# Forgetting attention's decay rows made once, and SBUF buffers moved to other addresses, in a three-block transformer kernel on one Trainium2 core

## The chip, the cores and the metric

The kernel runs on one core of a Trainium2 chip. The metric is the time of one execution on the device in microseconds (us), as a median of runs. TensorE (PE) has two levels of clock, 1.2 and 2.4 GHz; the profile shows which was granted. Beside it work VectorE (DVE), ScalarE (ACT), GpSimd (POOL) and the DMA queue of SyncE (SP).

## What is computed

One sequence of 256 tokens with 1024 channels passes through three transformer blocks in float32. Block A has dilated band attention of 16 heads, block B block-sparse causal attention (at 256 tokens plain causal attention), each followed by a gated MLP with a short convolution of width 3. Block C mixes three branches: forgetting attention with 8 heads of 64, a convolution branch, and a pooling branch. Each block ends with a gated MLP of width 2816. The part that the change rewrites is the decay in the forgetting attention:

```python
def forgetting_attention(q, k, v, fg_logit):
    log_f = jax.nn.log_sigmoid(fg_logit.astype(jnp.float32))
    cum = jnp.transpose(jnp.cumsum(log_f, axis=1), (0, 2, 1))
    ...
        s = jnp.einsum('bqhd,bkhd->bhqk', qb, kb).astype(jnp.float32) * ATT_SCALE
        s = s + cum[:, :, start:end, None] - cum[:, :, None, :end]
        s = jnp.where(ki <= qi, s, NEG)
        p = jax.nn.softmax(s, axis=-1).astype(vb.dtype)
```

The term of the query's own position is the same for all keys of a row and drops out of the softmax, so the kernel adds only minus the running sum over keys, per head.

## The kernel before

All weights arrive as 384 KB to 512 KB chunks of one stream, in the order of use, through a ring of six slots. ScalarE splits each chunk into a high part `w_hi` (`split_hi`, L362) and VectorE makes the rest `w_lo` (`split_lo`, L370), both in the type fp32r. A product of two float32 numbers is then three matmuls: high by high, low by high, high by low. The activations are split the same way: `xg` holds the normalised input's high and low halves side by side (x's split), `mix_hi` and `mix_lo` the branches' output, `g_hi` and `g_lo` (two buffers each) the gated product of the MLP.

Four kinds of matmul carry the kernel:

- the projections to queries, keys and values (`unit_chunk_pe`, L650 to L652): a slice of `xg` stands still, 384 columns of weights move;
- the MLP's up-projections (`project2_k`, L402 and L404): weights stand still, `xg` moves, 512 columns (both halves at once) and then 256. In the same step of the MLP follows
- the down-projection (L1707 to L1709): weights stand still, `g_hi`, `g_lo`, `g_hi` move, 256 columns each, 24 matmuls to a chunk;
- the output projections (L1189 to L1191), which have the same shape as the down-projection, with `mix_hi`, `mix_lo`, `mix_hi` moving.

The MLP's steps `j` alternate between two sets of buffers: an even step uses PSUM banks 0 and 1 and `g_hi0`, `g_lo0`, an odd one banks 2 and 3 and `g_hi1`, `g_lo1`. One step has 16 pairs of L402 and L404 and 24 matmuls of L1707 to L1709; there are 22 steps to an MLP and three MLPs.

The order of every engine's work is written out by hand. In block C, `att_c_pe`, `att_c_act` and `att_c_dve` walk through the 16 weight chunks n of the projections and hang the attention's work between them. `score_c_pe`, once for each of the four pairs of heads, first writes the decay into the score banks and then adds the scores (L763). Its core in the kernel before:

```python
        for h in range(2):
            for t in range(2):
                col = t * HEADS_C + 2 * pr + h
                ...
                for n, part in enumerate((fg_hi, fg_lo)):
                    nc.tensor.matmul(out, part[:, col:col + 1].broadcast_to([P, P]), tri[:, 0:3 * P - 2 * P * t],
```

One column of `fg_hi` (the logarithm of the forget gate, split into `fg_hi` and `fg_lo`), repeated 128 times, stands still, and the triangle `tri` of minus ones moves: 384 columns for the first 128 keys, 128 for the rest. That makes eight matmuls on L756 for a pair of heads.

Where a buffer lies in a partition of SBUF follows from the order and sizes in which the buffers are declared. The addresses in bytes modulo 1024 that matter here are, before: the weight slots 128 (all of them), `xg` and `mix_hi`, `mix_lo` 192, the four `g` buffers 256, and the attention's working buffers (`tokbuf`, `qkT`, `v_tok`, `prob`) 96 or 608.

Of the kernel before, what the change touches and what calls it, by code (L numbers as in the profile page):

```python
# [8 lines left out]
P = 128  # L9
D = 1024  # L10
TOK = 256
# [28 lines left out]
WARM_UP = 16  # L40
HALVES = 3
GAINS = 16
CHUNK = KT * P
UNIT = 3 * P
QCHUNK = 2 * UNIT
# [112 lines left out]
def build(nc, x_d, xa_d, stream_d, par_d, con_d, taps_d, out_d):  # L158
# [10 lines left out]
    def sem(name):  # L169
# [3 lines left out]
    w_raw = [sb(f"w_raw{s}", [P, CHUNK]) for s in range(RING)]  # L173
    w_hi = [sb(f"w_hi{s}", [P, CHUNK], F32R) for s in range(RING)]
    w_lo = [sb(f"w_lo{s}", [P, CHUNK], F32R) for s in range(RING)]
    x_all = sb("x_all", [P, GAINS + KT * TOK])
    xT = x_all[:, GAINS:GAINS + KT * TOK].rearrange("p (k t) -> p k t", t=TOK)
    xg = sb("xg", [P, KT, 2, TOK], F32R)
    xg_hi, xg_lo = xg[:, :, 0, :], xg[:, :, 1, :]
    mix_hi = sb("mix_hi", [P, KT, TOK], F32R)  # L180
# [1 line left out]
    par = sb("par", [P, N_PAR])  # L182
    con = sb("con", [P, N_CON])
    zero = sb("zero", [P, TOK], BF16)
    ln_x = sb("ln_x", [P, TOK])
    rms_r = sb("rms_r", [P, TOK])

# [34 lines left out]
    cv_h = [sb(f"cv_h{i}", [P, PADC + TOK + 2]) for i in range(2)]  # L222
    taps = sb("conv_taps", [P, N_TAPS])
    cv_s0 = sb("cv_s0", [P, SHIFTS * W_SHIFT])
    cv_shift = [[cv_s0[:, c * W_SHIFT:(c + 1) * W_SHIFT] for c in range(SHIFTS)],
                [v_tok[c][:, TOK:TOK + W_SHIFT] for c in range(3)] + [prob_t[:, 0, 2, 0:W_SHIFT]]]
    W_PL = POOL_PAD + TOK
# [27 lines left out]
    half_hi = sem("half_hi")  # L255
    half_lo = sem("half_lo")
    rest_in = sem("rest_in")
    pl_zeroed = sem("pl_zeroed")
    zeroed = sem("zeroed")
    acc_done = sem("acc_done")  # L260
    x_new = sem("x_new")
# [73 lines left out]
    fg_dve = sem("fg_dve")  # L335
    fg_act = sem("fg_act")
    fg_lo_done = sem("fg_lo_done")
    ln_pe = sem("ln_pe")
    ln_dve = sem("ln_dve")
    ln_act = sem("ln_act")  # L340
# [95 lines left out]
    def norm_gain(e, m):  # L436

        g = PAR_NORM + KT * e + m
        return x_all[:, m:m + 1] if e == 0 else par[:, g:g + 1]

    def first_hi_dve(eng):
        eng.wait_ge(x_first, 16)
# [284 lines left out]
    def score_pe(eng, st, pr, g):  # L727
# [10 lines left out]
                                        kk[lo:hi, g * TOK:g * TOK + (qt + 1) * P], start=True, stop=True)  # L738
        last.then_inc(a.score, 1)

    def score_c_pe(eng, pr):

        a, b = att[2], pr % 2
        q, kk = qkT[b]
        if pr > 0:
            eng.wait_ge(a.ptr, pr)
        else:
            eng.wait_ge(ln_act, 1)
        eng.wait_ge(tri_in, 1)
        eng.wait_ge(fg_lo_done, 1)  # L750
        for h in range(2):
            for t in range(2):
                col = t * HEADS_C + 2 * pr + h
                out = bank(S_BANK + h, 2 * P * t, 3 * P - 2 * P * t)
                for n, part in enumerate((fg_hi, fg_lo)):
                    nc.tensor.matmul(out, part[:, col:col + 1].broadcast_to([P, P]), tri[:, 0:3 * P - 2 * P * t],  # L756
                                     start=(t == 0 and n == 0), stop=False, skip_group_check=True)
        eng.wait_ge(a.qe, pr + 1)
        eng.wait_ge(a.ke, pr + 1)
        for qt in range(2):  # L760
            for h in range(2):
                lo, hi = HD * h, HD * h + HD
                last = nc.tensor.matmul(bank(S_BANK + h, qt * P, (qt + 1) * P), q[lo:hi, qt * P:(qt + 1) * P],  # L763
                                        kk[lo:hi, 0:(qt + 1) * P], start=False, stop=True, skip_group_check=True)
        last.then_inc(a.score, 1)
# [732 lines left out]
    def att_c_pe(eng):  # L1498
        for n in range(N_C):
            p, o = divmod(n, UCH)  # L1500
            unit_chunk_pe(eng, 2, n)
            if n == 1:
                conv_pe(eng, 0)
            if n == 2:
                conv_pe(eng, 1)
            if n == 3:
                ln_sum_pe(eng)
            if n == 4:
                ln_var_pe(eng)
            if o == 0 and p >= 3:  # L1510
                prob_t_pe(eng, 2, p - 3, 0)
            if o == 1 and p >= 2:
                score_c_pe(eng, p - 2)
            if o == 1 and p >= 3:
                pv_pe(eng, 2, p - 3)
            if n == 5:
                pool_mm_pe(eng)
            if n == N_C - 3:
                pw_pe(eng)
            if o == 3 and p >= 1:  # L1520
                if p == 1:
                    eng.wait_ge(side_lo, 2)
                if p == 3:
                    eng.wait_ge(side_lo, 4)
                qkt_pe(eng, 2, p - 1)
        p = PAIRS_C - 1
        out_first(eng, 2, 0, UPPER)
        prob_t_pe(eng, 2, p - 2, 0)
        out_first(eng, 2, 1, UPPER)
        score_c_pe(eng, p - 1)  # L1530
# [12 lines left out]
        out_first(eng, 2, 5, LOWER)  # L1543
        prob_t_pe(eng, 2, p, 0)
        out_first(eng, 2, 6, LOWER)
        pv_pe(eng, 2, p)
        out_second(eng, 2, 4, UPPER)
        out_first(eng, 2, 7, LOWER)
        out_second(eng, 2, 5, UPPER)
        out_second(eng, 2, 6, UPPER)  # L1550
        out_second(eng, 2, 7, UPPER)

    def att_c_act(eng):
        for n in range(N_C):
# [8 lines left out]
                prob_t_act(eng, 2, p - 3, 0)  # L1563
            if n == 5:
                ln_rsqrt_act(eng)
            if n == 8:
                forget_hi_act(eng)
            if o == 1 and p >= 1:
                norm_act(eng, 2, p - 1, 0, 4)
            if n == 6:  # L1570
# [37 lines left out]
    def att_c_dve(eng):  # L1608
        for n in range(N_C):
            p, o = divmod(n, UCH)  # L1610
            split_lo(eng, C_QKV + n + AHEAD)
            if n == 0:
                conv_shift_dve(eng, 1, 1)
# [4 lines left out]
            if n == 7:  # L1618
                forget_sigmoid_dve(eng)
            if n == 8:  # L1620
                forget_lo_dve(eng)
            if n == 4:
                ln_center_dve(eng)
            if o == 0 and p >= 1:
# [221 lines left out]
    def pre_act_f(eng):  # L1846

        for n in range(N_PRE):
            split_hi(eng, C_PRE + n + AHEAD_HI)
            if n == 2:  # L1850
                rows_act(eng, 4)
                cols_act(eng, 2)
                nc.scalar.activation(tri[:], con[:, CON_TRI:CON_TRI + 3 * P], ACT.Copy).then_inc(tri_in, 1)
            if n in (3, 5):
                t = n // 2 - 1
                eng.wait_ge(pre_out, 2 * t + 2)
                if t == 0:
                    nc.scalar.preload_act_table_set("sigmoid_and_others")
                nc.scalar.activation(cv_e[t], cv_b[t], ACT.Sigmoid).then_inc(pre_act, 1)
# [4 lines left out]
    def pre_dve_f(eng):  # L1864
# [6 lines left out]
        def out(n):  # L1871
            if n == 0:
                eng.wait_ge(x_r, ROW_NO[4])
            if n == 4:
                eng.wait_ge(pl_zeroed, 6)
            eng.wait_ge(tiles, C_PRE + n + 1)
            nc.vector.tensor_tensor(PRE_OUT[n], bank(PRE_BANK[n]), rms_r[:], ALU.mult).then_inc(pre_out, 1)

# [15 lines left out]
    def pool_zeroes(eng):  # L1894
        for t in range(2):
            for b in pl[t]:
                nc.gpsimd.memset(b, 0.0).then_inc(pl_zeroed, 1)

    def pre_pool_f(eng):

# [154 lines left out]
    with nc.Block() as block:  # L2055

        @block.sync
        def _(sp):
# [7 lines left out]
                sp.dma_start(w_raw[c][:, part], stream_d[c, :, part]).then_inc(half_in[c] if kk == 0 else w_loaded[c], 16)  # L2066

            def load_x(m, n, landed):
                part = slice(GAINS + m * TOK if m else 0, GAINS + (m + n) * TOK)
                sp.dma_start(x_all[:, part], xa_d[:, part]).then_inc(landed, 16)  # L2070

            load_x(0, 1, x_first)
            load_x(1, 1, x_in[0])
# [121 lines left out]
        def _(pool):  # L2195
            nc.gpsimd.memset(cv_h[0][:], 0.0).then_inc(zeroed, 1)
            nc.gpsimd.memset(cv_h[1][:], 0.0).then_inc(zeroed, 1)
            resid_pool(pool, 0)
            tables_pool(pool)
            att_a_pool(pool)  # L2200
# [166 lines left out]
```

## Time and profile before

| | |
|---|---|
| median of 3 runs | 1060.22 us (1059.83 to 1062.07) |
| profiled execution | 1060.19 us |
| its span | 1058.4 us |
| PE busy | 1053.8 us, 100% |
| PE weight loads busy | 981.7 us, 93% |
| DVE busy | 862.2 us, 81% |
| ACT busy | 685.9 us, 65% |
| POOL busy | 342.0 us, 32% |

The span goes from the first to the last instruction; 1.8 us of the execution lie around it. Matmuls overlap in the profile: an instruction's duration has its way through the array in it, so what one costs in a stream is read from the starts of two neighbours and not from its duration. Weight loads (PEld) run beside the matmuls.

### The profile page before, as it was taken

Reading aid. Unit: us, or ns where it says so; the run is one execution under the profiler, and the core shown is the slowest. Engines: PE = TensorE matmul, PEld = TensorE weight load, DVE = VectorE, ACT = ScalarE, POOL = GpSimd, SP = SyncE. Lnnn points to the kernel's source line nnn. Section 1 sums busy time; section 2 is a strip of 40 time slices with the busy share of each in tenths; the row PEclk is TensorE's granted clock in tenths of the full one; section 3 lists DMA queues with packets and bytes.
Section 4 is the critical chain, followed back from the end, with each engine's and each line's share of the span. In section 5 each row is a group of like instructions: output and inputs, shape, how many; then the busy total and the mean of one; then the engine's idle time right before and its main releaser. Section 6 shows DMA issues by size and latency. Waiting matters only on the chain.

```text
span 1058.4 us, 21208 instructions
## 1 busy us (share of the span) xinstructions
PE 1053.8 (100%) x7508; PEld 981.7 (93%) x7508; DVE 862.2 (81%) x1588; ACT 685.9 (65%) x1262; POOL 342.0 (32%) x368
## 2 busy tenths in 40 slices
PE   9999999999999999999999999999999999999998
PEld 8999999999999999999989899999998999999998
DVE  7877778877799888887777998888896769988886
ACT  7766676776766555576776665555686666655552
POOL 4312222121365333322122553333350025533331
PEclk9999999999999999999999999999999999999999
DMA  9644545455466555535453675555434436655541
GB/s 317 225 159 150 164 151 180 149 185 196 161 219 198 195 181 190 159 110 179 152 164 120 216 216 187 188 187 189 134 112 144 146 114 225 212 187 190 183 154 41
DMA packets 57749, 183.34 MB, mean 173 GB/s; under 512 B 6352, under 2 KB 9680, under 8 KB 57424
## 3 DMA queue, kind: packets, MB, share of 16 engines
q1 hardware_dynamic: 56816, 181.52, 52.7%
q8 instruction: 41, 0.67, 0.3%
q10 hardware_dynamic: 864, 0.92, 0.3%
q14 instruction: 28, 0.23, 0.1%
HBM read 181.36 MB, written 1.05 MB: 172 GB/s over the span
## 4 chain that ended last, share of the span: by engine, by line
PE 99%; DMA 0%; DVE 0%; ACT 0%; DVEq 0%; issue 0%
PE ps L402 23%; PE ps L404 12%; PE ps L650 10%; PE ps L652 9%; PE ps L651 9%; PE ps L1707 6%; PE ps L1709 6%; PE ps L1708 6%; PE ps L1189 2%; PE ps L1191 2%; PE ps L1190 2%; PE ps L584 1%; PE ps L809 1%; PE ps L854 1%; PE ps L783 1%; PE ps L821 1%
## 5 line engine op out<-in xcount | busy, mean ns | idle before, releaser
L370 DVE TENSOR_TENSOR w_lo<-w_raw,w_hi 128x1024 fp32r<-128x1024 f32 (+2 forms) x369 | 441.0, 1210 | 56.0 <-ACT w_hi L362 55.3
L362 ACT ACTIVATE w_hi<-w_raw 128x1024 fp32r<-128x1024 f32 (+2 forms) x369 | 354.1, 972 | 163.3 <-PE ps L404 136.6
L402 PE MATMUL ps<-xg,w_hi 128*128 128x512 f32 x1056 | 374.7, 396 | 0.0
L404 PE MATMUL ps<-xg,w_lo 128*128 128x256 f32 x1056 | 297.0, 281 | 0.0
L402 PEld LDWEIGHTS ps<-xg,w_hi 128*128 128x128 f32 x1056 | 198.6, 188 | 44.6
L404 PEld LDWEIGHTS ps<-xg,w_lo 128*128 128x128 f32 x1056 | 198.1, 188 | 0.1
L1829 POOL TENSOR_TENSOR prob_t<-prob_t,qkT 128x256 f32<-128x256 f32 x63 | 100.3, 1593 | 289.6 <-ACT prob_t L1752 289.6
L650 PE MATMUL ps<-w_hi,xg 128*128 128x384 f32 (+1 forms) x556 | 193.1, 347 | 0.0
L652 PE MATMUL ps<-w_hi,xg 128*128 128x384 f32 (+1 forms) x556 | 186.8, 336 | 0.0
L651 PE MATMUL ps<-w_lo,xg 128*128 128x384 f32 (+1 forms) x556 | 186.7, 336 | 0.0
L1707 PE MATMUL ps<-g_hi,w_hi 128*128 128x256 f32 x528 | 149.2, 283 | 0.0
L1709 PE MATMUL ps<-g_hi,w_lo 128*128 128x256 f32 x528 | 148.9, 282 | 0.0
L1708 PE MATMUL ps<-g_lo,w_hi 128*128 128x256 f32 x528 | 148.6, 281 | 0.0
L1823 POOL TENSOR_TENSOR qkT<-prob,rms_r 128x256 f32<-128x256 f32 x132 | 119.2, 922 | 19.0 <-DVE prob L1766 10.3
L1799 DVE SCALAR_TENSOR_TENSOR qkT<-qkT,par 128x255 f32<-128x255 f32 (+1 forms) x264 | 111.6, 476 | 4.3 <-ACT qkT L1745 4.2
L650 PEld LDWEIGHTS ps<-w_hi,xg 128*128 128x128 f32 x556 | 104.4, 188 | 3.4 <-issue 2.7
L651 PEld LDWEIGHTS ps<-w_lo,xg 128*128 128x128 f32 x556 | 104.5, 188 | 0.1
L652 PEld LDWEIGHTS ps<-w_hi,xg 128*128 128x128 f32 x556 | 104.3, 188 | 0.0
L1707 PEld LDWEIGHTS ps<-g_hi,w_hi 128*128 128x128 f32 x528 | 99.6, 189 | 2.7
L1745 ACT ACTIVATE qkT<-qkT,par 128x256 f32<-128x256 f32 x132 | 76.4, 597 | 37.6 <-POOL qkT L1823 37.4
L1708 PEld LDWEIGHTS ps<-g_lo,w_hi 128*128 128x128 f32 x528 | 99.7, 189 | 0.0
L1709 PEld LDWEIGHTS ps<-g_hi,w_lo 128*128 128x128 f32 x528 | 99.3, 188 | 0.0
(182 smaller groups left out, 1388.5 us busy)
## 6 DMA issues: line engine op xcount, KB each, us to landing
w_raw<-w_stream SPq DMA_DIRECT2D x228, 512.0 KB, 3.6
w_raw<-w_stream SPq DMA_DIRECT2D x137, 384.0 KB, 3.4
w_raw<-w_stream SPq DMA_DIRECT2D x4, 392.0 KB, 3.0
con<-consts SPq DMA_DIRECT2D x1, 1024.0 KB, 7.5
x_all<-x_t SPq DMA_DIRECT2D x4, 256.0 KB, 5.5
conv_taps<-taps SPq DMA_DIRECT2D x1, 1024.0 KB, 7.1
w_raw<-w_stream SPq DMA_DIRECT2D x4, 192.0 KB, 4.4
x_all<-x_a SPq DMA_DIRECT2D x3, 256.0 KB, 5.5
```

The source lines that it names most:

```text
L362: nc.scalar.activation(w_hi[s][:, 0:w], w_raw[s][:, 0:w], ACT.Copy).then_inc(w_hi_done, 1)
L370: nc.vector.tensor_tensor(w_lo[s][:, 0:w], w_raw[s][:, 0:w], w_hi[s][:, 0:w].bitcast(F32), ALU.subtract).then_inc(w_lo_done, 1)
L402: nc.tensor.matmul(bank(b, 0, 2 * TOK), w_hi[s][:, k * P:(k + 1) * P], xg[:, k, :, :].rearrange("p h t -> p (h t)"), start=(k == 0), stop= ...
L404: last = nc.tensor.matmul(bank(b), w_lo[s][:, k * P:(k + 1) * P], xg_hi[:, k, :], start=False, stop=(k == KT - 1), skip_group_check=True)
L650: nc.tensor.matmul(out, hi, wh, start=(k == 0), stop=False)
L651: nc.tensor.matmul(out, hi, wl, start=False, stop=False)
L652: last = nc.tensor.matmul(out, lo, wh, start=False, stop=(k == KT - 1))
L1707: nc.tensor.matmul(acc(m), wh, g_hi[b][:], start=first, stop=False, skip_group_check=True)
L1708: nc.tensor.matmul(acc(m), wh, g_lo[b][:], start=False, stop=False, skip_group_check=True)
L1709: last = nc.tensor.matmul(acc(m), wl, g_hi[b][:], start=False, stop=True, skip_group_check=True)
L1799: nc.vector.scalar_tensor_tensor(cv_s[b][s][:, k:TOK], up_s[b][s][:, 0:TOK - k], par_col(f, t, per, i, 4 * s + 2 - k), cv_s[b][s][:, k:TOK ...
L1823: nc.gpsimd.tensor_tensor(up_s[t % 2][s], up_sum[s], rms_r[:], ALU.mult).then_inc(F.up, 1)
```

## The change

Three things are done.

1. **Addresses.** `x_all` is declared larger (its contents start at 960 bytes into it), and an unused buffer `gap` of 736 bytes is declared after `zero`. The new buffers stand at the end. Modulo 1024, `xg`, `mix_hi` and `mix_lo` move from 192 to 128, the four `g` buffers from 256 to 928, the attention's working buffers from 96 or 608 to 768 or 256, `par` from 192 to 128, `con` from 64 to 0, `tri` from 256 to 928. The weight slots stay at 128.
2. **Decay.** `decay_pe`, at chunk n = 8, makes the eight heads' running sums once, as eight rows of 384 columns in bank `K_BANK`: a block of eight columns of `fg_hi` or `fg_lo` stands still and `tri` moves. ACT copies them to `decay_hi` (fp32r), DVE makes the rest `decay_lo`. `score_c_pe` then picks a head's row with `head_row`, the first eight columns of the identity, one of which is repeated 128 times and stands still while all 384 columns of `decay_hi` and then `decay_lo` move: four matmuls for a pair of heads.
3. **Order.** `forget_hi_act` moves from n = 8 to n = 7 on ACT and `forget_lo_dve` to the front of n = 8 on DVE; `decay_act` and `decay_dve` come in at n = 8. Two memsets of 128x384 stand at POOL's start, one small copy (`head_row`) in ACT's work before block C's attention, and the semaphore `pl_zeroed` is merged into `zeroed`.

The diff, cut to its core:

```diff
+X0 = TOK
+GAP = 184
-    x_all = sb("x_all", [P, GAINS + KT * TOK])
-    xT = x_all[:, GAINS:GAINS + KT * TOK].rearrange("p (k t) -> p k t", t=TOK)
+    x_all = sb("x_all", [P, X0 + KT * TOK])
+    xT = x_all[:, X0:X0 + KT * TOK].rearrange("p (k t) -> p k t", t=TOK)
     zero = sb("zero", [P, TOK], BF16)
+    sb("gap", [P, GAP])
     cv_s0 = sb("cv_s0", [P, SHIFTS * W_SHIFT])
+    head_row = sb("head_row", [P, HEADS_C], F32R)
+    decay_hi = sb("decay_hi", [P, 3 * P], F32R)
+    decay_lo = sb("decay_lo", [P, 3 * P], F32R)
+    def decay_pe(eng):
+
+        eng.wait_ge(tri_in, 1)
+        eng.wait_ge(fg_lo_done, 1)
+        eng.wait_ge(att[2].ke, 1)
+        for t in range(2):
+            for n, part in enumerate((fg_hi, fg_lo)):
+                last = nc.tensor.matmul(bank(K_BANK, 2 * P * t, 3 * P - 2 * P * t)[0:HEADS_C, :],
+                                        part[:, t * HEADS_C:(t + 1) * HEADS_C], tri[:, 0:3 * P - 2 * P * t],
+                                        start=(t == 0 and n == 0), stop=False, skip_group_check=True)
+        last.then_inc(decay, 1)
+
+    def decay_act(eng):
+        eng.wait_ge(decay, 1)
+        eng.wait_ge(zeroed, 4)
+        nc.scalar.activation(decay_hi[0:HEADS_C, :], bank(K_BANK, 0, 3 * P)[0:HEADS_C, :], ACT.Copy).then_inc(decay, 1)
+
+    def decay_dve(eng):
+        eng.wait_ge(decay, 2)
+        nc.vector.tensor_tensor(decay_lo[0:HEADS_C, :], bank(K_BANK, 0, 3 * P)[0:HEADS_C, :],
+                                decay_hi[0:HEADS_C, :].bitcast(F32), ALU.subtract).then_inc(decay, 1)
     def score_c_pe(eng, pr):
-        eng.wait_ge(tri_in, 1)
-        eng.wait_ge(fg_lo_done, 1)
+        eng.wait_ge(decay, 3)
         for h in range(2):
-            for t in range(2):
-                col = t * HEADS_C + 2 * pr + h
-                out = bank(S_BANK + h, 2 * P * t, 3 * P - 2 * P * t)
-                for n, part in enumerate((fg_hi, fg_lo)):
-                    nc.tensor.matmul(out, part[:, col:col + 1].broadcast_to([P, P]), tri[:, 0:3 * P - 2 * P * t],
-                                     start=(t == 0 and n == 0), stop=False, skip_group_check=True)
+            col = 2 * pr + h
+            for n, part in enumerate((decay_hi, decay_lo)):
+                nc.tensor.matmul(bank(S_BANK + h, 0, 3 * P), head_row[:, col:col + 1].broadcast_to([P, P]), part[:],
+                                 start=(n == 0), stop=False, skip_group_check=True)
```

On PE, after the projections' chunk n = 9 (L650 to L652 before), the first pair of heads' decay stands like this in the kernel before:

```order
L652 MATMUL ps<-w_hi,xg 128x384
L756 MATMUL ps<-tri,fg_hi 128x384
L756 MATMUL ps<-tri,fg_lo 128x384
L756 MATMUL ps<-tri,fg_hi 128x128
L756 MATMUL ps<-tri,fg_lo 128x128
L756 MATMUL ps<-tri,fg_hi 128x384
L756 MATMUL ps<-tri,fg_lo 128x384
L756 MATMUL ps<-tri,fg_hi 128x128
L756 MATMUL ps<-tri,fg_lo 128x128
L763 MATMUL ps<-qkT 128x128 x2
L763 MATMUL ps<-qkT 128x256 x2
```

In the changed kernel (whose L656 to L658 are the projections) the same place and, before it, the end of chunk n = 8 read:

```order
L658 MATMUL ps<-w_hi,xg 128x384
L754 MATMUL ps<-tri,fg_hi 8x384
L754 MATMUL ps<-tri,fg_lo 8x384
L754 MATMUL ps<-tri,fg_hi 8x128
L754 MATMUL ps<-tri,fg_lo 8x128
L656 MATMUL ps<-w_hi,xg 128x384
...
L781 MATMUL ps<-decay_hi,head_row 128x384
L781 MATMUL ps<-decay_lo,head_row 128x384
L781 MATMUL ps<-decay_hi,head_row 128x384
L781 MATMUL ps<-decay_lo,head_row 128x384
L788 MATMUL ps<-qkT 128x128 x2
```

Eight matmuls for a pair have become four, and four have come in once, a chunk earlier.

On DVE, between the keys of pair 0 and the norms of pair 1, the kernel before has (L370 the weights' split, L1004 and L1018 the norms):

```order
L1033 TENSOR_SCALAR qkT<-ps,gain_qk 128x256
L370 TENSOR_TENSOR w_lo<-w_raw,w_hi 128x768
L991 TENSOR_TENSOR fg_lo<-fg,fg_hi 128x16
L1004 TENSOR_REDUCE ss_q<-tokbuf 128x4 x2
L370 TENSOR_TENSOR w_lo<-w_raw,w_hi 128x768
L1018 SCALAR_TENSOR_TENSOR tokbuf<-ps,r_c,r_q 128x256 x2
```

And the changed kernel:

```order
L1058 TENSOR_SCALAR qkT<-ps,gain_qk 128x256
L1016 TENSOR_TENSOR fg_lo<-fg,fg_hi 128x16
L376 TENSOR_TENSOR w_lo<-w_raw,w_hi 128x768
L766 TENSOR_TENSOR decay_lo<-ps,decay_hi 8x384
L1029 TENSOR_REDUCE ss_q<-tokbuf 128x4 x2
L376 TENSOR_TENSOR w_lo<-w_raw,w_hi 128x768
L1043 SCALAR_TENSOR_TENSOR tokbuf<-ps,r_c,r_q 128x256 x2
```

The small `fg_lo` has moved ahead of a split, and `decay_lo` stands ahead of the sums. ACT changes likewise: its `fg_hi` copy moves up by one chunk, and `decay_hi` takes its old place.

## Rows read from the trace of the kernel before

**Rows 1.** The page: span, busy time, share and instructions of engines, granted clock, chain.

```profile
span 1058.4 us, 21208 instructions
PE 1053.8 (100%) x7508; PEld 981.7 (93%) x7508; DVE 862.2 (81%) x1588; ACT 685.9 (65%) x1262; POOL 342.0 (32%) x368
...
PEclk9999999999999999999999999999999999999999
...
PE 99%; DMA 0%; DVE 0%; ACT 0%; DVEq 0%; issue 0%
```

**Rows 2.** Groups on PE by form: busy us, mean ns of one, idle before.

```profile
L650 PE MATMUL ps<-w_hi,xg 128*128 128x384 f32 x540 | 187.5, 347 | 0.0
...
L1707 PE MATMUL ps<-g_hi,w_hi 128*128 128x256 f32 x528 | 149.2, 283 | 0.0
...
L1189 PE MATMUL ps<-mix_hi,w_hi 128*128 128x256 f32 x192 | 55.5, 289 | 0.0
```

**Rows 3.** Timeline of PE at pair 0's decay: start us, us, what.

```profile
815.03 0.34 PE L756 MATMUL ps<-tri,fg_hi 128*128 128x384 f32 x1
815.21 0.33 PE L756 MATMUL ps<-tri,fg_lo 128*128 128x384 f32 x1
815.38 0.22 PE L756 MATMUL ps<-tri,fg_hi 128*128 128x128 f32 x1
815.44 0.27 PE L756 MATMUL ps<-tri,fg_lo 128*128 128x128 f32 x1
815.55 0.39 PE L756 MATMUL ps<-tri,fg_hi 128*128 128x384 f32 x1
...
816.22 0.93 PE L763 MATMUL ps<-qkT 64*128 64x128 f32 x8
```

**Rows 4.** Timeline of ACT in block C's attention.

```profile
776.14 0.51 ACT L1853 ACTIVATE tri<-con 128x384 fp32r<-128x384 f32 x1
...
811.15 0.85 ACT L362 ACTIVATE w_hi<-w_raw 128x768 fp32r<-128x768 f32 x1
...
813.43 0.64 ACT L893 ACTIVATE v_tok<-ps,r_c 128x128 f32<-128x128 f32 x2
813.93 0.24 ACT L987 ACTIVATE fg_hi<-fg 128x16 fp32r<-128x16 f32 x1
814.04 0.87 ACT L362 ACTIVATE w_hi<-w_raw 128x768 fp32r<-128x768 f32 x1
...
818.63 0.40 ACT L950 ACTIVATE prob<-prob,nmax 128x128 f32<-128x128 f32 x1 [2.17 <-DVE nmax L1094]
```

**Rows 5.** Timeline of DVE in the same stretch.

```profile
812.03 0.96 DVE L370 TENSOR_TENSOR w_lo<-w_raw,w_hi 128x768 fp32r<-128x768 f32 x1 [0.49 <-ACT w_hi L362]
...
814.30 0.74 DVE L1004 TENSOR_REDUCE ss_q<-tokbuf 128x4 f32<-128x256 f32 x2
...
817.19 0.29 DVE L1087 CUSTOM_DVE_ANT_0 prob<-ps,con 128x128 f32<-128x128 f32 x1 [0.50 <-PE ps L763]
```

**Rows 6.** Windows of the first MLP: ups, down, ups, down of two steps.

```profile
305.11:310.77 5.66, 5.66 (x35) 4.93 (x34) 5.39 (x9) 2.99 (x6) 3.77 (x3) 1.00 0.76 224
310.77:313.64 2.87, 2.87 (x26) 2.87 (x25) 2.87 (x5) 2.13 (x3) 1.54 (x1) 1.00 0.40 134
313.64:319.24 5.60, 5.60 (x35) 4.90 (x33) 5.35 (x9) 3.53 (x6) 2.83 (x3) 1.00 0.78 260
319.24:322.08 2.84, 2.84 (x27) 2.84 (x25) 2.84 (x4) 1.68 (x3) 2.39 (x2) 1.00 0.42 131
```

**Rows 7.** Timeline of PE in block B's output projection.

```profile
553.40 0.28 PE L1190 MATMUL ps<-mix_lo,w_hi 128*128 128x256 f32 x1
...
556.01 0.60 PE L723 MATMUL ps<-con,tokbuf 128*128 128x128 f32 x4
```

**Rows 8.** Timeline of PE in block C's output projection.

```profile
852.84 0.28 PE L1189 MATMUL ps<-mix_hi,w_hi 128*128 128x256 f32 x1
...
857.79 0.82 PE L840 MATMUL ps<-con,prob 128*128 128x128 f32 x6
```

More of the change, by code:

```diff
@@ L257, in build @@
     rest_in = sem("rest_in")
-    pl_zeroed = sem("pl_zeroed")
     zeroed = sem("zeroed")
@@ L337, in build @@
     fg_lo_done = sem("fg_lo_done")
+    decay = sem("decay")
     ln_pe = sem("ln_pe")
@@ L438, in norm_gain @@
         g = PAR_NORM + KT * e + m
-        return x_all[:, m:m + 1] if e == 0 else par[:, g:g + 1]
+        return x_all[:, X0 - GAINS + m:X0 - GAINS + m + 1] if e == 0 else par[:, g:g + 1]
     def first_hi_dve(eng):
@@ L1517, in att_c_pe @@
                 pool_mm_pe(eng)
+            if n == 8:
+                decay_pe(eng)
             if n == N_C - 3:
@@ L1565, in att_c_act @@
                 ln_rsqrt_act(eng)
+            if n == 7:
+                forget_hi_act(eng)
             if n == 8:
-                forget_hi_act(eng)
+                decay_act(eng)
             if o == 1 and p >= 1:
@@ L1610, in att_c_dve @@
             p, o = divmod(n, UCH)
+            if n == 8:
+                forget_lo_dve(eng)
             split_lo(eng, C_QKV + n + AHEAD)
@@ L1620, in att_c_dve @@
             if n == 8:
-                forget_lo_dve(eng)
+                decay_dve(eng)
             if n == 4:
@@ L1852, in pre_act_f @@
                 cols_act(eng, 2)
+                nc.scalar.activation(head_row[:], con[:, CON_ID:CON_ID + HEADS_C], ACT.Copy)
                 nc.scalar.activation(tri[:], con[:, CON_TRI:CON_TRI + 3 * P], ACT.Copy).then_inc(tri_in, 1)
@@ L1874, in out @@
             if n == 4:
-                eng.wait_ge(pl_zeroed, 6)
+                eng.wait_ge(zeroed, 10)
             eng.wait_ge(tiles, C_PRE + n + 1)
@@ L1896, in pool_zeroes @@
             for b in pl[t]:
-                nc.gpsimd.memset(b, 0.0).then_inc(pl_zeroed, 1)
+                nc.gpsimd.memset(b, 0.0).then_inc(zeroed, 1)
     def pre_pool_f(eng):
@@ L2068, in load_x @@
             def load_x(m, n, landed):
-                part = slice(GAINS + m * TOK if m else 0, GAINS + (m + n) * TOK)
-                sp.dma_start(x_all[:, part], xa_d[:, part]).then_inc(landed, 16)
+                a, b = GAINS + m * TOK if m else 0, GAINS + (m + n) * TOK
+                sp.dma_start(x_all[:, X0 - GAINS + a:X0 - GAINS + b], xa_d[:, a:b]).then_inc(landed, 16)
             load_x(0, 1, x_first)
@@ L2197, in _ @@
             nc.gpsimd.memset(cv_h[1][:], 0.0).then_inc(zeroed, 1)
+            nc.gpsimd.memset(decay_hi[:].bitcast(F32), 0.0).then_inc(zeroed, 1)
+            nc.gpsimd.memset(decay_lo[:].bitcast(F32), 0.0).then_inc(zeroed, 1)
             resid_pool(pool, 0)
```

## The prediction

> **What bounds the kernel now.** The page first: PE is busy for 1053.8 of 1058.4 us, the chain that ended last is PE for 99%, and the granted clock is in the top tenth (2.4 GHz) in every slice [rows 1]. Nothing that another engine does sets the time unless it makes PE wait. So only two things can move it: which matmuls PE has, and how far apart they start. For the second, durations are no use (283 ns for a 256-column matmul of L1707, [rows 2]), since they overlap; starts are. In the first MLP, 24 down matmuls take 2.87 us in one step and 2.84 us in the next, 119.6 and 118.3 ns each, and the 16 pairs of up matmuls 5.66 and 5.60 us, 353.8 and 350.0 ns a pair [rows 6]. 256 columns at 2.4 GHz are 106.7 ns, so each down matmul carries 12 to 13 ns beyond its columns; a pair's 768 columns are 320 ns, and it carries 30 to 34 ns. Over the program that is some 20 us in the down matmuls (three MLPs times 22 steps times 24 are 1584) and some 34 us in the 1056 pairs. These are what an address could touch.
>
> **The change part by part, the decay.** Before, pair 0's eight decay matmuls start at 815.03 and the scores at 816.22: 1.19 us; the first four steps are 0.18, 0.17, 0.06 and 0.11 us [rows 3]. The new block has four of 384 columns. Three steps at 0.175 make 0.525 us; the last step, into the scores, whose stationary operand sits on half the rows, costs more than its columns: before it was the eighth of the block, and what the first seven leave of 1.19 us (0.52 for the first four, some 0.46 for the next three, whose first starts at 815.55) is 0.21 us for a 128-column matmul. With 384 columns instead I add the 0.107 us of 256 columns at least nothing (if the load of the weights sets that step) and at most all of it: 0.21 to 0.32, I take 0.27. The block is then 0.80 us, against 1.19: 0.39 saved, four times: 1.6 us, between 1.4 and 1.8.
>
> The four new `decay_pe` matmuls have the same columns as the first four of the old block, with only eight columns of weights to load: 0.52 us by those rows, 0.43 (1024 columns at 2.4 GHz) at the least. Net of the decay: minus 1.1 us, bounds minus 0.9 to minus 1.4.
>
> **The waits it adds.** `score_c_pe` waits for `decay_lo` on DVE, which waits for `decay_hi` on ACT, which waits for PE. Worked forward: chunk n = 9 runs for twelve matmuls of 384 columns, 2.1 us at 0.174, up to 815.03, so n = 8 ends at 812.95. `fg_hi` now follows the split that begins at 811.15 and takes 0.85 [rows 4], so it is there at 812.2 and `fg_lo` at 812.4, 0.5 us ahead of `decay_pe`. That ends at 813.45 plus 0.2 of its own way through the array. ACT is at its v copies until 814.0 then, and puts `decay_hi` where the 0.11 us of `fg_hi` were; a 128x384 copy took 0.51 us at L1853 [rows 4]: 814.5. DVE is idle from there for nothing else; a 128x768 subtraction took 0.96 [rows 5], so 384 columns about 0.55: 815.1. Chunk 9 ends 0.5 us later than before, at 815.5. PE has 0.4 us in hand. I cost the wait at nothing; if both copies ran as long as their 768-column rows (0.85 and 0.96) it would be short by some 0.3 us, once.
>
> Behind these two instructions things slide. DVE's sums, before at 814.30 [rows 5], come at 815.1; the split behind them and the norms then end some 0.8 to 0.9 us later, and the masks, which before started at 817.19 after 0.50 us of idle time, start near 817.6. ACT's exponentials, which had waited 2.17 us for that maximum [rows 4], begin 0.4 us later. The split now late is that for chunk 12, which PE reaches after 821, and ACT and DVE have idle time in between. Nothing on PE. The memsets at POOL's start and the 0.1 us of `head_row` on ACT lie under work that PE does not wait for.
>
> **The change part by part, the addresses.** No instruction is added, so only the steps between starts can change. What bears on whether they depend on an address: the output projections have the same shape as the down matmuls, three matmuls of 256 columns on two weight loads of the same slots, and differ in that their moving operand lies at 192 modulo 1024, the MLP's at 256. In block C, 42 of them take 4.95 us, 117.9 ns each [rows 8]; in block B 23 take 2.61 us, 113.5 ns each [rows 7]. Two rates at one address: so history (how the stream was entered) sets it too. The up pairs also alternate between 353.8 and 350.0 ns at one address of x. But of the triples, those at 256 are the slowest on record, at 119.6 and 118.3, and this is the address given up. The 1620 projection matmuls of L650 to L652 (540 of L650, [rows 2]) move weights, which stay at 128, and only hold x still; I leave them alone.
>
> What 928 gives no row shows. The nearest rows are the other triples. If `g` ran at block C's 117.9, 1584 matmuls would save 1.1 ns each, 1.7 us; at block B's 113.5, 8.6 us; if all steps ran as the even ones, at 119.6, they would cost 1.0 us. I take 117.7, nearer the first row because it is twice as long and the next to the MLP in time: minus 2.0 us. For x at 128, all pairs at 350.0 would save 2.0 us, all at 353.8 would cost 2.0; I take nothing. Of the output projections (192 triples, 576 matmuls) nothing either, with bounds of 1 us each way.
>
> **The sum.** Against the profiled execution, 1060.19 us, of which 1058.4 are the span: minus 1.1 for the decay, minus 2.0 for the gated product: 1057.1 us. The median of the runs is 1060.22, so the same holds there.
>
> **The rivals.**
> (a) Only the decay is worth anything: the addresses don't reach PE. For it: two rates at one address, as above, and the MLP's pattern is as regular as if only the code set it. Time 1059.1. The Trainium skill has a rule for this case: its page "SBUF — State Buffer", section "Who interferes with whom", says that PE never waits on another engine, and "TensorE: Matmul & The Clock Gate", section "Step-by-step: what each phase is for", that the moving operand and the weight load have independent read ports. By these an address could not matter at all, and the sum would be this rival's.
> (b) The new addresses are slower. Two streams, moving and stationary, are read side by side; before, `g` stood 128 bytes above the weights modulo 1024 and x 64; now x stands level with them, and 928 is the only one that isn't a multiple of 64. If the pairs settle at 353.8 or above and the triples at 119.6 or above, that is 2.0 and 1.0 us; with each step 2 ns more besides, 5 us more. The time would be 1061 to 1067; it decides against me from 3.1 us of added steps, about 1.2 ns on each of the 2640 up steps and down matmuls. For it: nothing but that both are untried.
> (c) Both become faster: the pairs at 350.0 throughout and the triples at 115 or so, minus 2.0 and minus 6.4: 1050.7; for it the 113.5 in block B, against it that no MLP step shows it.
> (d) PE waits for `decay_lo`: a gap of up to 1 us in front of the first decay block, and the decay's gain is gone, 1058 to 1060 with the rest as it falls.
>
> **Chances and range.** A faster gated product, x unchanged: 0.42. (a): 0.26. (b): 0.18. (c): 0.10. (d): 0.04. What a measurement of this kernel can tell from no change is about 0.2%, 2.1 us. Faster by more than that are the forecast, nearly all of it, and (c): 0.51. Within are (a), (d) and a bit of (b): 0.32. Slower: 0.17. The range that leaves out 2 in 10 is 1052 to 1062.5 us: below it most of (c), above it most of (b). The forecast's own range is 1055 to 1058.1.
>
> **What would show it.** In the changed profile: the decay block four matmuls in 0.8 us from first start to the scores, `decay_pe` in 0.5, and no idle step ahead of either. In the MLPs, the 24 down matmuls of a step should take 2.80 to 2.84 us in place of 2.87 and 2.84, and the 16 pairs still 5.66 and 5.60. The prediction is wrong if the steps of the down matmuls stand as they were (then (a)), if the pairs move by more than 0.05 us a step, or if the first decay block is preceded by a gap.

## The result, and the profile after

The changed kernel takes 1054.28 us (median of 6 runs, 1054.01 to 1054.57), against 1061.21 us for the kernel before (6 runs, 1059.83 to 1062.57): ratio 0.9939, 95% interval 0.9929 to 0.9949. The profiled execution took 1054.57 us, its span 1052.8 us, 5.6 us less than before. The forecast was 1057.1 in a range of 1052.0 to 1062.5. Of the six runs of the kernel before, three took 1059.8 to 1060.4 us and three 1062.1 to 1062.6, while those of the changed kernel lie within 0.6 us; the profiled execution before is one of the faster three, which is why the medians are 6.9 us apart and the spans 5.6.

The page of the kernel after (span; busy time and share of each engine; granted clock in 40 slices; shares of the chain that ended last):

```profile
span 1052.8 us, 21191 instructions
PE 1047.9 (100%) x7496; PEld 977.1 (93%) x7496; DVE 864.5 (82%) x1589; ACT 687.4 (65%) x1264; POOL 345.0 (33%) x370
...
PEclk9999999999999999999999999999999999999999
...
PE 97%; DMA 1%; DVE 1%; ACT 0%; POOL 0%; issue 0%; SPq 0%; DVEq 0%; POOLq 0%
```

Against [rows 1], PE is still busy throughout, at the same granted clock in every slice (2.4 GHz), and its busy time fell by 5.9 us, as the span did by 5.6. The other engines do slightly more. PE's matmuls are only 12 fewer, so most of the gain must be in their spacing. The windows of two steps of the first MLP, pairs then down matmuls, show where (columns: window, length, busy time of PE, PEld, DVE, ACT and POOL, granted clock, DMA share, GB/s):

```profile
322.60:328.15 5.55, 5.55 (x34) 4.89 (x33) 5.30 (x8) 3.65 (x6) 2.41 (x3) 1.00 0.70 238
328.15:330.98 2.83, 2.83 (x26) 2.83 (x25) 2.83 (x5) 1.49 (x3) 2.75 (x3) 1.00 0.55 188
330.98:336.53 5.55, 5.55 (x34) 4.89 (x33) 5.31 (x8) 3.40 (x5) 2.48 (x2) 1.00 0.54 187
336.53:339.36 2.83, 2.83 (x26) 2.83 (x25) 2.83 (x4) 1.97 (x3) 2.75 (x3) 1.00 0.82 275
```

In [rows 6] the same windows were 5.66, 2.87, 5.60 and 2.84. The pairs, which the forecast left as they were, lost 0.11 and 0.05 us a step (346.9 ns a pair now), the down matmuls 0.04 and 0.01 (117.9 ns each), and the two steps no longer differ.

A matmul's cost is the time from its start to the next one's. Summed over each group (the small ones are left out):

| group (us) | before | after | change | forecast |
|---|---|---|---|---|
| up pairs (`project2_k`) | 372.06 | 367.87 | −4.19 | 0, bounds ±2.0 |
| down matmuls | 188.46 | 186.70 | −1.76 | −2.0 |
| block C's decay and scores (`score_c_pe`) | 8.15 | 6.58 | −1.57 | −1.6 |
| `decay_pe` | 0 | 0.47 | +0.47 | +0.52 |
| output projections | 70.04 | 71.30 | +1.26 | 0, bounds ±1 |
| block C's `project_k` (x moving, triples) | 18.36 | 18.63 | +0.27 | not named |
| projections with x at rest (`unit_chunk_pe`) | 298.68 | 298.74 | +0.06 | 0 |
| all matmuls | 1053.88 | 1048.25 | −5.63 | −3.1 |

The +0.06 of the projections with x at rest is made of two parts. Their last matmul ahead of block A's first transposes takes 0.46 us longer, because PE waits there for GpSimd, and all the others together take 0.40 us less:

```profile
29.99 0.87 PE L703 MATMUL ps<-con,tokbuf 128*128 128x128 f32 x6 [0.30 <-POOL tokbuf L1184]
```

The output projections are the group that lost most; on PE's timeline (start, duration, what), a matmul of block C's and the one that starts 45 steps later:

```profile
848.39 0.28 PE L1215 MATMUL ps<-mix_lo,w_hi 128*128 128x256 f32 x1
...
853.78 0.28 PE L1215 MATMUL ps<-mix_lo,w_hi 128*128 128x256 f32 x1
```

That is 5.39 us for 45 steps, 119.8 ns each, where [rows 8] gave 117.9: these matmuls, whose moving operand now lies level with the weights, run as slowly as the down matmuls did before.

The decay, on PE:

```profile
810.19 0.34 PE L754 MATMUL ps<-tri,fg_hi 128*8 128x384 f32 x1
810.36 0.33 PE L754 MATMUL ps<-tri,fg_lo 128*8 128x384 f32 x1
810.53 0.22 PE L754 MATMUL ps<-tri,fg_hi 128*8 128x128 f32 x1
810.59 0.22 PE L754 MATMUL ps<-tri,fg_lo 128*8 128x128 f32 x1
...
812.79 0.34 PE L781 MATMUL ps<-decay_hi,head_row 128*128 128x384 f32 x1
812.96 0.34 PE L781 MATMUL ps<-decay_lo,head_row 128*128 128x384 f32 x1
813.14 0.33 PE L781 MATMUL ps<-decay_hi,head_row 128*128 128x384 f32 x1
813.31 0.34 PE L781 MATMUL ps<-decay_lo,head_row 128*128 128x384 f32 x1
813.58 0.93 PE L788 MATMUL ps<-qkT 64*128 64x128 f32 x8
```

The block takes 0.79 us up to the scores (1.19 in [rows 3]), and no idle time is noted ahead of it. The load of its first weights and ACT's and DVE's parts of the same chain:

```profile
812.61 0.19 PEld L781 LDWEIGHTS ps<-decay_hi,head_row 128*128 128x128 f32 x1
```

```profile
811.27 0.46 ACT L762 ACTIVATE decay_hi<-ps 8x384 fp32r<-8x384 f32 x1
```

```profile
811.77 0.55 DVE L766 TENSOR_TENSOR decay_lo<-ps,decay_hi 8x384 fp32r<-8x384 f32 x1 [1.35 <-ACT decay_hi L762]
```

`decay_lo` is ready at 812.32. The block's first matmul starts at 812.79, but PE's wait stands in the program ahead of the matmul and its weight load, and that load starts at 812.61: 0.29 us in hand. DVE idles 1.35 us ahead of `decay_lo`, and no idle time of PE follows from it.

### The profile page after: what moved, and what is told of

Its sections match the earlier page's. It is cut to its first block, busy times and chain, and to the rows that moved or that the text cites. A ratio compares the mean times of both kernels' runs of the same rounds, so it can differ in the third digit from the quotient of the medians.

```text
span 1052.8 us, 21191 instructions
## 1 busy us (share of the span) xinstructions
PE 1047.9 (100%) x7496; PEld 977.1 (93%) x7496; DVE 864.5 (82%) x1589; ACT 687.4 (65%) x1264; POOL 345.0 (33%) x370
## 4 chain that ended last, share of the span: by engine, by line
PE 97%; DMA 1%; DVE 1%; ACT 0%; POOL 0%; issue 0%; SPq 0%; DVEq 0%; POOLq 0%
PE ps L408 23%; PE ps L410 12%; PE ps L656 9%; PE ps L658 9%; PE ps L657 9%; PE ps L1738 6%; PE ps L1739 6%; PE ps L1740 6%; PE ps L1214 2%; PE ps L1215 2%; PE ps L1216 2%; DMA w_raw<-w_stream 1%; PE ps L834 1%; PE ps L879 1%; PE ps L808 1%; PE ps L846 1%
## 5 line engine op out<-in xcount | busy, mean ns | idle before, releaser
L368 ACT ACTIVATE w_hi<-w_raw 128x1024 fp32r<-128x1024 f32 (+2 forms) x369 | 353.8, 972 | 152.6 <-PE ps L410 128.5
L408 PE MATMUL ps<-xg,w_hi 128*128 128x512 f32 x1056 | 370.4, 393 | 0.0
L656 PE MATMUL ps<-w_hi,xg 128*128 128x384 f32 (+1 forms) x556 | 192.6, 346 | 0.0
L658 PE MATMUL ps<-w_hi,xg 128*128 128x384 f32 (+1 forms) x556 | 186.4, 335 | 0.0
L656 PEld LDWEIGHTS ps<-w_hi,xg 128*128 128x128 f32 x556 | 104.5, 188 | 3.4 <-issue 2.7
L658 PEld LDWEIGHTS ps<-w_hi,xg 128*128 128x128 f32 x556 | 104.4, 188 | 0.0
```

The costliest lines, as they stand in the source:

```text
L368: nc.scalar.activation(w_hi[s][:, 0:w], w_raw[s][:, 0:w], ACT.Copy).then_inc(w_hi_done, 1)
L408: nc.tensor.matmul(bank(b, 0, 2 * TOK), w_hi[s][:, k * P:(k + 1) * P], xg[:, k, :, :].rearrange("p h t -> p (h t)"), start=(k == 0), stop= ...
L656: nc.tensor.matmul(out, hi, wh, start=(k == 0), stop=False)
L658: last = nc.tensor.matmul(out, lo, wh, start=False, stop=(k == KT - 1))
```

## The experiments

Positions below are bytes modulo 256 unless said otherwise; the weights stand at 128 if nothing else is said. After the result two questions are open: why the pairs moved, and whether what counts is where an operand lies or how far it lies from the other operand.

### The decay alone, and the addresses alone

`e1_decay` is the kernel before with all of the decay's edits and before's positions:

```diff
+X0 = GAINS
-    x_all = sb("x_all", [P, GAINS + KT * TOK])
+    x_all = sb("x_all", [P, X0 + KT * TOK])
...
+    head_row = sb("head_row", [P, HEADS_C], F32R)
+    decay_hi = sb("decay_hi", [P, 3 * P], F32R)
+    decay_lo = sb("decay_lo", [P, 3 * P], F32R)
```

> The decay rows alone, all buffers at the addresses of the kernel before. Sums are over the time from each matmul's start to the next one's start. Theory A (each kind of matmul stream has its own step, set by where its moving operand lies modulo 1024): score_c's matmuls with decay_pe fall by 1.1 us as in the changed kernel, up pairs stay at 372 us, down matmuls at 188.5, output projections at 70.0; ratio to before 0.999. Theory B (the phase of the stream is history, and any change of the program redraws it): up pairs and down matmuls move too, by 1 to 4 us. Theory C (the decay's new order on ACT and DVE brought part of the gain): ratio below 0.997.

`e2_addr` is the kernel before with the positions alone:

```diff
+X0 = TOK
+GAP = 184
...
     zero = sb("zero", [P, TOK], BF16)
+    sb("gap", [P, GAP])
```

> The addresses of the changed kernel with the decay of the kernel before. If the two parts add up: 1.1 us slower than the changed kernel, ratio to before 0.995; up pairs 368, down 186.7, output projections 71.3 us. If the new addresses only pay together with the new order: ratio above 0.997.

The decay alone: 1059.13 us, ratio 0.9994 (0.9985 to 1.0003), span 1057.1 against 1058.4. The interval takes in 1, so the time alone doesn't show this gain; PE's groups do. Its pairs take 372.01 us, its down matmuls 188.46, its output projections 70.02, all as before; `score_c_pe` 6.58 and `decay_pe` 0.47. The addresses alone: 1055.23 us, ratio 0.9951 (0.9937 to 0.9964), span 1053.6; pairs 367.92, down 186.70, output projections 71.32, `score_c_pe` 8.15. The spans are 1.3 and 4.8 us shorter, 6.1 in sum, where both parts together gave 5.6. The groups named here add up, each to within 0.1 us. Four fifths of the gain are the addresses.

### One distance at a time

`e3_x` keeps the new position of x and puts `g` back to 256 modulo 1024, that is 0 (x and mix lie ahead of `gap` and don't move with its size; the attention's working buffers and `tri` lie behind it and go back too):

```diff
-GAP = 184
+GAP = 16
```

> The changed kernel with the gap cut to 64 bytes: x's split and the mixed branches stay at 128 modulo 1024, the gated product and the attention's working buffers go back to 256 and 96. Theory A: up pairs stay at 368 us (before 372), output projections at 71.3 (before 70.0), down matmuls go back to 188.5 from 186.7; time 1.8 us above the changed kernel, ratio to before 0.9955. Theory B: up pairs at some third value. Theory D (the up pairs gained through the working buffers' or the gated product's addresses, since they follow the down matmuls and take over their phase): up pairs back at 372 and ratio 0.999.

`e4_g` has x and mix at 192 as before and `g` at 928 modulo 1024, that is 160:

```diff
-X0 = TOK
-GAP = 184
+X0 = GAINS
+GAP = 168
```

> The changed kernel with x's split and the mixed branches back at 192 modulo 1024, the gated product at 928 and the working buffers at 768 as in the changed kernel. Theory A: up pairs at 372 us, output projections at 70.0, down matmuls 186.7 as in the changed kernel; ratio to before 0.9975. Theory B: a third value for each. Theory D: up pairs at 368, ratio 0.994.

`e3_x` took 1060.73 us, ratio 1.0003 (0.9994 to 1.0012): the gain was gone, where the first theory had expected 0.9955. Its windows of pairs and down matmuls:

```profile
322.43:328.08 5.65, 5.65 (x35) 4.90 (x33) 5.40 (x9) 3.46 (x6) 2.50 (x3) 1.00 0.70 215
328.08:330.93 2.85, 2.85 (x27) 2.85 (x26) 2.85 (x4) 1.81 (x3) 2.77 (x3) 1.00 0.64 217
```

x's pairs stood at the new position and ran at 5.65, not at 5.55; over the program they took 372.95 us, 0.88 more than before. In the first steps of the MLP, ahead of the loop, they had run at 5.55 here too and then changed to 5.65. `e4_g` took 1057.83 us, ratio 0.9974 (0.9965 to 0.9983):

```profile
322.13:327.79 5.66, 5.66 (x35) 4.93 (x34) 5.40 (x9) 3.49 (x6) 2.51 (x3) 1.00 0.72 237
327.79:330.59 2.80, 2.80 (x27) 2.80 (x25) 2.80 (x4) 1.73 (x3) 2.72 (x3) 1.00 0.59 199
```

Its down matmuls were faster than after's (184.92 against 186.70 us in all), its pairs the slowest (373.93), where the first theory had 186.7 and 372. So neither stream has a cost that goes by its own position alone: of these four kernels only the one with x at 128 and `g` at 160 runs its pairs at 5.55, and what `g` at 160 gives depends on where x is. My reading, that the two moves could be costed apart, fell here.

### Distance or position

`e6_all64` moves everything by 64 bytes, weights too (weights 192, x 192, `g` 992):

```diff
+    sb("gap_all", [P, 16])
```

> The changed kernel with 64 unused bytes ahead of the first buffer, so that every buffer, the weights too, lies 64 bytes higher: x's split 192, gated product 992, weights 192. If distances between the streams' operands count: up pairs 368 us, down 186.7, output 71.3, ratio to before 0.994. If absolute addresses modulo 1024 count: up pairs 372 to 374, ratio 0.998 to 1.000.

It took 1054.08 us, ratio 0.994 (0.9927 to 0.9954), and three of PE's groups are those of the kernel after to the last digit: pairs 367.87, down 186.70, output projections 71.30.

```profile
322.07:327.62 5.55, 5.55 (x34) 4.89 (x33) 5.30 (x8) 3.66 (x6) 2.41 (x3) 1.00 0.77 248
327.62:330.45 2.83, 2.83 (x26) 2.83 (x25) 2.83 (x5) 1.49 (x3) 2.75 (x3) 1.00 0.48 181
```

x stands at 192 here, where it stood in the kernel before, and runs at 5.55. What counts is how the operands lie to each other and not where they lie; that was tested with this one shift.

`e5_mix` is after with mix back at 64 bytes above the weights, the rest as after:

```diff
-GAP = 184
+GAP = 168
+    sb("gap_mix", [P, 16])
```

> The changed kernel with a gap of 64 bytes ahead of the mixed branches: they lie at 192 modulo 1024 as in the kernel before, x's split at 128 and the gated product at 928. Theory A: output projections back from 71.3 to 70.0 us and all else as in the changed kernel, 1.3 us below it, ratio to before 0.9925. Theory B: up pairs or down matmuls move as well.

1053.39 us, ratio 0.9934 (0.992 to 0.9948), span 1051.8, 1.0 below after's. The output projections are back at 69.99 us, the pairs at 368.12 and the down matmuls at 186.61; `unit_chunk_pe` took 299.21, 0.47 more than after, of which 0.12 is the wait for GpSimd ahead of block A's first transposes; the rest nothing here explains. The change's largest loss was mix's move, and it can be undone by itself.

### PE alone

Four kernels leave the transformer out and have PE go through the MLP's streams with nothing beside it, on fixed buffers filled once. Each was executed once. Each case, that is each set of positions, begins with a matmul of four columns (`kick`). The core of the first three:

```python
            for xo, go in CASES:
                kick(xo)
                for j in range(STEPS):
                    pairs(xo, 2 * (j % 2), 0)
                    pairs(xo, 2 * (j % 2) + 1, 1)
                    down(go, j % 2, j % 2)
```

`map_g` has x at 128 and `g` at 0 to 992 modulo 1024 in steps of 32.

> PE alone: the kernel leaves the whole computation out and returns x. It runs the MLP's two streams (16 up pairs, 24 down matmuls a step, four steps) 32 times, x at 128 modulo 1024 and the gated product at 0, 32, ... 992, weights at 128, no other engine at work. Theory A' (the two streams' addresses and nothing else set the steps): at 928 a step has its up pairs in 5.55 us and down in 2.83, at 256 in 5.65 and 2.85, as the MLPs of the changed kernel and of the one with g back at 256. Rival (other engines' reads and writes of SBUF make the extra time): up pairs near 5.2 and down near 2.62 at every address, which is their columns plus 2.5 ns a matmul.

`map_x` has `g` at 928 modulo 1024 and x at 0 to 992.

> The same kernel, gated product at 928, x at 0, 32, ... 992 modulo 1024 (whole computation left out). Theory A': at 192 the pairs take 5.66 us a step and down 2.80, at 128 5.55 and 2.83. If only the distance from the weights (128) matters the values repeat in some pattern of 64 or 128 bytes. Rival: no dependence.

The page of `map_g` shows that nothing but PE works:

```profile
PE 1088.3 (98%) x7241; PEld 998.2 (90%) x7241; ACT 10.2 (1%) x9; POOL 0.2 (0%) x4
```

And its windows of one step each with `g` at 64, 256, 320 and 928 modulo 1024 (columns: window, length, busy time of PE, granted clock, DMA share, GB/s):

```profile
114.34:119.90 5.56, 5.56 (x35) 1.00 0.00 0
119.90:122.62 2.72, 2.72 (x26) 1.00 0.00 0
317.39:323.05 5.66, 5.66 (x35) 1.00 0.00 0
323.05:325.89 2.84, 2.84 (x26) 1.00 0.00 0
384.73:390.28 5.55, 5.55 (x34) 1.00 0.00 0
390.28:393.01 2.73, 2.73 (x26) 1.00 0.02 6
1026.92:1032.47 5.55, 5.55 (x35) 1.00 0.01 3
1032.47:1035.30 2.83, 2.83 (x27) 1.00 0.00 0
```

At 928 it gives after's 5.55 and 2.83, at 256 `e3_x`'s 5.65 and 2.85 to 0.01 us, without any other engine. So neither the other engines nor the working buffers that moved with `g` are needed for the effect. Adding 256 bytes changes nothing (64 and 320). The last step of each case, ns from the first start of a part to the next part's:

```
position of the one that varies      0    32    64    96   128   160   192   224
map_g (x at 128): 16 pairs        5653  5639  5554  5547  5651  5552  5649  5552
                  24 down         2847  2819  2726  2835  2882  2828  2828  2881
map_x (g at 928): 16 pairs        5600  5552  5651  5546  5551  5547  5657  5600
                  24 down         2815  2801  2829  2808  2829  2800  2803  2827
```

(Some cases alternate from step to step, and the last step stands here: the step before, `map_g` at 32 had pairs at 5552, at 192 down at 2721, and `map_x` at 96 had pairs at 5644. For `map_x` at 0 the middle of two values stands here: 5608 and 2805 at 0 modulo 1024, 5595 and 2825 at 256, 512 and 768.)

`map_xg` takes eight positions of x times eight of `g`, three steps each.

> PE alone (whole computation left out, returns x): x and gated product each at the eight multiples of 32 in 256 bytes, three steps for each of the 64 cases. If each stream has a time of its own, a row and a column of the first two maps predict every cell: x at 128 pairs 5.55, gated product at 64 down 2.73, and no cell below 8.25 us a step. If the streams hand over a phase to each other, cells with the same gated product differ in their down time by 0.02 to 0.1 us.

Its windows of the third step for (x, g) = (32, 64), (160, 64) and (192, 0), the last being the kernel before's:

```profile
303.51:309.08 5.57, 5.57 (x41) 1.00 0.00 0
309.08:311.81 2.73, 2.73 (x18) 1.00 0.00 0
1117.61:1123.17 5.56, 5.56 (x41) 1.00 0.00 0
1123.17:1125.99 2.82, 2.82 (x20) 1.00 0.02 6
1269.48:1275.14 5.66, 5.66 (x40) 1.00 0.00 0
1275.14:1278.01 2.87, 2.87 (x20) 1.00 0.00 0
```

The down matmuls at one position of `g` take 2.73 after x at 32 and 2.82 after x at 160: a stream's rate also depends on the one that it follows. Of the 64 combinations x at 128 with `g` at 64 is the least in the third step, 8280 ns; the largest is 8536. The kernel before's combination has 8535 there, but 8432 in the second step: pairs and down matmuls take 5657 and 2878 ns in the one and 5594 and 2838 in the other. These are the two kinds of step of [rows 6] (5.66 and 2.87, 5.60 and 2.84), so PE alone shows both kinds of step, at one position of x and of `g`.

`map_m` runs the triples of the down matmuls alone, then uniform streams of 256, 384 and 512 columns with new weights for each matmul, then the projections' stream with x at rest. In a triple the first two matmuls have the same weights, but PE loads weights for each of the three (`map_g`'s page counts as many loads as matmuls, 7241).

> PE alone (whole computation left out, returns x), eight positions of the moving operand in 256 bytes: the triple of the down matmuls by itself, uniform streams of 256, 384 and 512 columns with one new load of weights for each matmul, and the projections' stream, where weights move and x holds still. If the extra time comes from the moving operand's distance to the weights being loaded, the triple by itself takes 113 to 114 ns a matmul at 64 and 118 to 120 at 128, and the uniform streams vary with position too; the projections' stream does as well, since the distance is the same seen from the other side. If it comes from the moving operand's own alignment, the projections' stream is the same at all eight.

Windows of 24 matmuls of the triples with `g` at 64 (the first two), 128 and 160:

```profile
136.89:139.61 2.72, 2.72 (x26) 1.00 0.00 0
139.61:142.33 2.72, 2.72 (x26) 1.00 0.00 0
236.78:239.66 2.88, 2.88 (x26) 1.00 0.00 0
285.36:288.16 2.80, 2.80 (x26) 1.00 0.00 0
```

ns for one matmul, by position of `g` or x, with the weights at 128:

```
position                   0      32      64      96     128     160     192     224
above the weights by     128     160     192     224       0      32      64      96
triples, 256 columns   120.0   118.6   113.3   118.3   120.0   116.7   117.8   120.0
uniform, 256           118.6   117.4   117.8   118.4   120.0   116.6   117.8   119.9
uniform, 384           176.4   176.7   173.4   173.3   173.3   176.6   173.3   176.7
uniform, 512           232.2   234.3   233.3   233.4   226.7   233.3   228.9   233.2
x at rest, 384         176.0   176.7   173.3   173.3   173.3   173.3   174.7   173.3
```

The triples keep such a value step after step, but another start of the same stream can settle on another one: with `g` at 64 it took 2826 ns per 24 at another start (2720 at the first), at 0 it took 2849 (2880). The two rates that the forecast noted at one address in [rows 7] and [rows 8], 113.5 and 117.9 ns, look like this. The full kernels show it too: with mix at 192 in all three, 48 matmuls in a row of block B's output projection took 115.7 ns each in `e5_mix`, as in the kernel before, and the same 48 took 119.9 in `e4_g`.

### The positions that the map prefers

`e7_best` leaves x at 128 and puts mix and `g` at 64 (the working buffers move along, to 160):

```diff
-GAP = 184
+GAP = 176
+    sb("gap_mix", [P, 48])
```

> The changed kernel with the mixed branches at 64 and the gated product at 64 modulo 256 (x stays at 128, weights at 128). If the map of PE alone holds in the full kernel (period 256 bytes, down matmuls in 2.73 us a step instead of 2.83 where the gated product lies at 64, up pairs 5.55): down matmuls 180 us instead of 186.7, output projections, which are the same triple, 68 instead of 71.3, up pairs 368; time 1044, ratio to before 0.985. Rival (the changed kernel's addresses are good because of 928 or of the working buffers that moved with them, and the map doesn't carry over with other engines at work): 1054 or above.

1047.63 us (4 runs, 1047.6 to 1048.57), ratio 0.9881 (0.9864 to 0.9897): faster than both kernels, 6.6 us below after. Its windows of a step:

```profile
322.14:327.70 5.56, 5.56 (x35) 4.90 (x33) 5.30 (x9) 3.70 (x6) 2.61 (x3) 1.00 0.73 262
327.70:330.43 2.73, 2.73 (x27) 2.73 (x26) 2.73 (x4) 1.61 (x3) 2.36 (x2) 1.00 0.39 134
```

Down matmuls took 180.47 us in all, 6.2 less than after, and output projections 68.69, 2.6 less. The time missed the expectation of 1044 by 3.6 us, and part of that is a new wait. On the weight loads' timeline at the start of the third MLP:

```profile
861.36 0.19 PEld L409 LDWEIGHTS ps<-xg,w_hi 128*128 128x128 f32 x1 [0.37 <-DVE xg L474]
...
862.41 0.19 PEld L409 LDWEIGHTS ps<-xg,w_hi 128*128 128x128 f32 x1 [0.40 <-DVE xg L474]
...
863.65 0.19 PEld L409 LDWEIGHTS ps<-xg,w_hi 128*128 128x128 f32 x1 [0.59 <-DVE xg L474]
```

PE comes to the MLP before VectorE has made x's low halves. The waits' summary has six such waits:

```profile
PEld ps L409 <- DVE xg L474: 2.7, 6, 0.6
```

From the first pair of the second and of the third MLP to the next step's first pair it takes 7.03 us in place of 5.90, so 2 times 1.13 us are lost there; without them the pairs' 369.91 us would be 367.65. Against the kernel after, `unit_chunk_pe` took 0.57 us more (299.31 us), of which 0.35 is the wait for GpSimd ahead of block A's first transposes. Against the expected 368, 180 and 68, the pairs (with these waits), the down matmuls and the output projections are 1.9, 0.5 and 0.7 us too long; with the projections' 0.57 that makes the 3.6. But the trace is that of the slowest of the four executions, 1 us above the other three, and no trace shows what those did otherwise.

## Why the prediction was right, and where a step of it failed

**What bounds the kernel.** Right: PE is the chain for 97%, and the time between its matmuls' starts fell by 5.63 us in sum, as the span did by 5.6.

**The decay.** Right: block of 0.79 us (0.80 forecast), `decay_pe` 0.47 (0.52), net −1.1 (−1.1), and −1.1 again on PE's groups in `e1_decay`. The wait for `decay_lo` cost nothing, as forecast; counted to the weight load it had 0.29 us in hand and not 0.4. Rival (d) did not come.

**The gated product.** −1.76 against −2.0, at 117.9 ns in place of the 117.7 that I chose from block C's row. The size was right by luck: it was taken from a row with its moving operand 64 bytes above the weights, and `g` went to 32 above; by `e4_g` the same address of `g` gives 2.80 us a step (116.7 ns) with x at 192. The working also says that a triple has two weight loads, where the page of the kernel before has as many loads as matmuls (7508); the sum doesn't use it.

**x's pairs.** This is the term that failed: costed at nothing, with bounds of 2.0 us each way taken from the two rates of [rows 6]; they gave −4.2. But for the first steps of each MLP's loop, the pairs now run below both of those rates (346.9 ns against 350.0 and 353.8). The bound was wrong in kind: two rates seen at one distance say nothing about another distance. It was also wrong to cost the streams one by one, as `e3_x` and `e4_g` show. By the prediction's own sign (wrong if the pairs move by more than 0.05 us a step) this part of it was wrong: the even steps moved by 0.11.

**The output projections.** Costed at nothing with bounds of 1 us, +1.26: just outside, for the same reason. `e5_mix` takes it back with mix alone.

**The sum.** −3.1 forecast, −5.6 measured. What was not in the forecast is pairs −4.2, output projections +1.3, `project_k` +0.3, and the gated product is 0.2 short. The errors partly cancel, and the time stayed in the range of 1052 to 1062.5; it lies below the forecast's own range, which ended at 1055. The direction was right, but the largest part of the size, the pairs' −4.2, came from a term that stood at nothing, so that the time is in the range is in part luck.

**The rivals.** (a), that addresses do not reach PE, is refuted by `e2_addr` (−4.8 us of span with no instruction added or taken out) and by the maps. The Trainium skill says on its page "SBUF — State Buffer", section "Who interferes with whom", that the ports for the matmul's moving operand and for the weight load are independent. For these fp32r streams it can't be concluded from this, as (a) did, that an address doesn't matter: the step depends on where the two operands lie to each other, 113.3 to 120.0 ns for 256 columns. Whether the ports themselves are independent no run here shows. The same section says that PE never waits on another engine. Of the access to SBUF, which that section is about, the trace agrees for the MLP's steps: PE alone has the same 5.55 and 2.83 us as in the full kernel. (b) put its doubt on x standing level with the weights; with `g` at 160 that is a good place for the pairs (5.55 us), and for the triples one of the worst (120.0 ns in `map_m`), which is what the output projections met. (c) had the right sign for both streams; it put the pairs at 350.0 ns and the triples at 115, and they came to 346.9 and 117.9.

**What stays open.** Shown is that the spacing goes with how the two operands lie to each other, with a period of 256 bytes, in PE alone; that it is the distance, and not the position, rests on `e6_all64`'s one shift of 64 bytes. Only multiples of 32 bytes were tried. Which part of the hardware makes it so was not measured, nor why a stream can settle on more than one value, nor why half of the kernel before's runs took 2 us more.

## What to carry to other kernels

Where PE is the chain from end to end, divide a regular stretch of matmuls by their count of starts: if the steps differ between places that have the same shape, try where the moving buffers lie against the weights, modulo 256 bytes, with an unused buffer of 16 to 48 words, and measure all streams that alternate together and not one by one. Price such a move by measuring PE's stream alone and not from the rates seen at other distances. Then look at the start of each stage, since PE, once faster, can find the next engine's work not ready.

## What the runs showed of the hardware

- At 2.4 GHz (granted clock 1.00), fp32r matmuls with new weights followed at 116.6 to 120.0 ns for 256 columns, 173.3 to 176.7 for 384, 226.7 to 234.3 for 512, by the distance of the moving operand from the stationary one; in triples, where two of three matmuls have the same weights, 256 columns had 113.3 to 120.0.
- The period is 256 bytes: `map_g` gives the same values at 64 and at 320 (5.55 and 2.73 us).
- Moving both operands by 64 bytes changes nothing (`e6_all64`: pairs 367.87 us, as after).
- With weights moving and x at rest it is seen as well, 173.3 to 176.7 ns for 384 columns (`map_m`).
- A stream's rate depends on the one that it follows (2.73 and 2.82 us for the same 24 matmuls in `map_xg`), and the same stream can settle on two rates at one distance (2720 and 2826 ns per 24 in `map_m`).
- PE loads weights for each matmul, also where the next one has the same weights: 7241 loads for 7241 matmuls in `map_g`.
